# Two gate projections turned token-major, weight units placed by 64 bytes, and three steps of the attention stage reordered, in a two-layer hybrid decoder trunk

## The reference

```
y_mla   = attention of latents (softmax, causal), v 128 wide a head
y_mlstm = sigmoid(mo) * head_norm(h_ml, mlstm_norm_g)      # mo: 512 columns of z
y_ret   = silu(rg)    * head_norm(h_rt, ret_norm_g)        # rg: 512 columns of z
merged  = sum over the 3 branches b of gate[b] * (y_b @ w_br_b)
out     = merged @ w_out
```

## Time and profile before

| | us |
|---|---|
| median of 3 runs | 1314.21 |
| lowest, highest | 1313.94, 1314.42 |
| the profiled execution | 1314.52 |
| its span, first to last instruction | 1312.2 |

### The profile page before, as it was taken

One profiled execution on the slowest core, in us unless ns is written; L12 is line 12 of the kernel. 1 busy time (PEld: TensorE's weight loads), 2 busy tenths in 40 slices (PEclk: granted clock), 3 DMA queues, 4 the chain that ended last, 5 costly groups with the idle time before them and its releaser, 6 DMA issues.

```text
span 1312.2 us, 19330 instructions
## 1 busy us (share of the span) xinstructions
PE 1299.0 (99%) x8365; PEld 1178.1 (90%) x8365; DVE 889.7 (68%) x1078; ACT 637.9 (49%) x654; POOL 69.5 (5%) x59
## 2 busy tenths in 40 slices
PE   8999999999999999999999999999999999999998
PEld 8888889999999998888898888899999998988886
DVE  6666667998755676556675666779976656766555
ACT  5444446585534354444454444456754344544441
POOL 0398000000000000000000000000000000000000
PEclk9999999999999999999999999999999999999999
DMA  8755556544556555555556655556445564555562
GB/s 292 239 187 184 187 185 176 181 128 131 161 191 191 164 173 181 192 192 192 165 188 192 192 189 187 166 165 193 129 129 173 181 193 161 181 187 185 188 193 94
DMA packets 180341, 234.85 MB, mean 179 GB/s; under 512 B 7905, under 2 KB 154977, under 8 KB 180129
## 3 DMA queue, kind: packets, MB, share of 16 engines
q1 hardware_dynamic: 179872, 231.78, 55.5%
q0 software_dynamic: 240, 1.71, 0.4%
q10 hardware_dynamic: 144, 0.13, 0.1%
HBM read 232.56 MB, written 1.05 MB: 178 GB/s over the span
## 4 chain that ended last, share of the span: by engine, by line
PE 94%; DVE 3%; ACT 2%; issue 0%; DMA 0%; DVEq 0%
PE ps L1429 22%; PE ps L1418 22%; PE ps L1344 10%; PE ps L1343 10%; PE ps L1342 10%; PE ps L1417 10%; PE ps L1407 5%; PE ps L1421 1%; DVE wlo L802 1%; PE ps L1364 1%; PE ps L1376 1%; ACT whi L511 1%; PE ps L1624 1%; DVE ml_qk L974 0%; ACT rot_sw L597 0%; ACT sc L611 0%
## 5 line engine op out<-in xcount | busy, mean ns | idle before, releaser
L802 DVE TENSOR_TENSOR wlo<-raw,whi 128x2048 fp32r<-128x2048 f32 (+1 forms) x218 | 491.9, 2272 | 191.1 <-ACT whi L511 191.0
L511 ACT ACTIVATE whi<-raw 128x2048 fp32r<-128x2048 f32 (+1 forms) x218 | 413.2, 1897 | 293.8 <-DMA raw<-ffn_w_gate 113.4
L1418 PE MATMUL ps<-xpair,whi 128*128 128x512 f32 x1216 | 423.9, 395 | 0.0
L1417 PE MATMUL ps<-xpair,wlo 128*128 128x256 f32 x1064 | 299.2, 281 | 0.0
L1342 PE MATMUL ps<-xpair,whi 128*128 128x256 f32 (+1 forms) x928 | 261.5, 282 | 0.0
L1344 PE MATMUL ps<-xpair,wlo 128*128 128x256 f32 (+1 forms) x928 | 259.3, 279 | 0.0
L1343 PE MATMUL ps<-xpair,whi 128*128 128x256 f32 (+1 forms) x928 | 259.1, 279 | 0.0
L1418 PEld LDWEIGHTS ps<-xpair,whi 128*128 128x128 f32 x1216 | 221.1, 188 | 42.1
L1417 PEld LDWEIGHTS ps<-xpair,wlo 128*128 128x128 f32 x1064 | 199.6, 188 | 7.0
L1343 PEld LDWEIGHTS ps<-xpair,whi 128*128 128x128 f32 (+1 forms) x928 | 173.9, 187 | 0.5
L1342 PEld LDWEIGHTS ps<-xpair,whi 128*128 128x128 f32 (+1 forms) x928 | 173.7, 187 | 0.3
(11 more groups left out here) (234 smaller groups left out, 1572.1 us busy)
## 6 DMA issues: line engine op xcount, KB each, us to landing
raw<-w_in SPq DMA_DIRECT2D x60, 1024.0 KB, 5.2
raw<-ffn_w_down SPq DMA_DIRECT2D x44, 1024.0 KB, 4.9
raw<-ffn_w_gate SPq DMA_DIRECT2D x43, 1024.0 KB, 5.4
raw<-ffn_w_up SPq DMA_DIRECT2D x43, 1024.0 KB, 5.4
raw<-w_br SPq DMA_DIRECT2D x12, 1024.0 KB, 5.0
raw<-w_out SPq DMA_DIRECT2D x8, 1024.0 KB, 4.9
raw<-mla_w_uq SPq DMA_DIRECT2D x4, 576.0 KB, 3.9
raw<-mla_w_ukv SPq DMA_DIRECT2D x2, 1024.0 KB, 4.8
```

The lines of the kernel that those rows point to most:

```text
L511: act.activation(whi[:, n % RING, 0:size_of(n)], raw[:, n % RING, 0:size_of(n)], ACT.Copy).then_inc(w_hi, 1)
L802: dve.tensor_tensor(w_low(n), raw[:, n % RING, 0:size_of(n)], whi[:, n % RING, 0:size_of(n)].bitcast(F32), ALU.subtract).then_inc(w_lo, 1)
L1417: pe.matmul(ps[:, bank, 0:SEQ], wl[:, kk, cols], xhi[:, kk, :], start=False, stop=False)
L1418: last = pe.matmul(ps[:, bank, :], wh[:, kk, cols], xpair[:, kk, :, :], start=kk == 0, stop=kk == KC - 1)
```

## The change

1. `raw`/`wlo` and `whi` become flat rings with 64 bytes to spare, and a function gives each unit an offset of 0 or 64 bytes (`SHIFT`, 16 floats). The operands that were set 64 bytes off (`hhi` and its like, and `mhi`) lose their offsets, so that all of x's parts lie at 0 modulo 128; `raw` and `whi` begin at 64 as before. An offset of 64 bytes puts a unit at 0. It is given to the mixer's units 0, 1, 16 to 21 and 40 to 43, and to all FFN units but the first two of each layer.
2. As a shifted unit reaches 64 bytes into the next slot, some loads wait for unit n-4 instead of n-5: seven in each layer, FFN unit 5 and mixer units 17, 18, 19, 40, 42, 43.
3. mo and rg are projected token-major, each as two halves of the rows, with the sigmoid and the silu after the second half. The gate is multiplied into `hn` before the turn, and after it `gain_out` multiplies by the gain and splits, straight from PSUM.
4. In the attention stage `qn1` is copied before the rope part is swapped, and the values of token tile 1 come before those of tile 0; `pt_copy(0)` and `pt_copy(1)` go ahead of the silu; `lo(m0 + 16)` goes behind `rotate(2)`.

```diff
-LINE = 64
+LINE, ROW, SHIFT = 64, 512, 16
...
-    r_raw = region(4 * RING * UNIT)
-    raw, wlo = place("raw", [P, RING, UNIT], F32, r_raw), place("wlo", [P, RING, UNIT], F32R, r_raw)
-    whi = sb("whi", [P, RING, UNIT], F32R)
-    region(LINE)
+    r_raw = region(4 * RING * UNIT + ROW)
+    raw, wlo = (place(name, [P, RING * UNIT + SHIFT], dt, r_raw) for name, dt in (("raw", F32), ("wlo", F32R)))
+    whi = sb("whi", [P, RING * UNIT + SHIFT], F32R)
...
-    hhi = place("hhi", [P, 2 * SEQ], F32R, r_u2 + 448 + 4096)
+    hhi = place("hhi", [P, 2 * SEQ], F32R, r_u2 + 4096)
...
-    mlo = place("mlo", [P, KC, SEQ], F32R, r_y + LINE + 12288)
+    mlo = place("mlo", [P, KC, SEQ], F32R, r_y + 12288)
...
+    def shift_of(n):
+
+        k = n % U_LAYER - MIX_BASE
+        if 0 <= k < U_MIX:
+            return SHIFT if k < 2 or 16 <= k < MIX_FIXED or k >= U_MIX - MIX_OUT else 0
+        return 0 if k in (-MIX_BASE, 1 - MIX_BASE) else SHIFT
+
+    def unit(ring, n, lo=0, size=None):
+
+        at_n = n % RING * UNIT + shift_of(n) + lo
+        return ring[:, at_n:at_n + (size or size_of(n))]
+
+    def freed_by(n):
+
+        meets_next = n % RING < RING - 1 and shift_of(n) > shift_of(n - RING + 1)
+        return n - RING + 1 if meets_next else n - RING
...
-                sp.wait_ge(w_used, done_no(n - RING))
+                sp.wait_ge(w_used, done_no(freed_by(n)))
...
-                    if c == C_RV:
+                    if c in (C_RV, C_MO, C_RG):
                         load_half(l, m + i, c, i)
...
             act.wait_ge(w_used, done_no(m0 + 10))
+            copy(flat(q_nope[:, 2:4, :]), "qn1").then_inc(q_copied, 1)
             act.wait_ge(rotated, l * 6 + 1)
             swap("qr", 32).then_inc(rot_copied, 1)
-            copy(flat(q_nope[:, 2:4, :]), "qn1").then_inc(q_copied, 1)
...
+            pt_copy(0)
+            pt_copy(1)
             act.wait_ge(conv_tap, l * 32 + 32)
             act.activation(ml_qk[:, 4:8, :], ml_qk[:, 4:8, :], ACT.Silu).then_inc(qk_silu, 1)
 
-            pt_copy(0)
-            pt_copy(1)
...
             hi(m0 + 22)
-            act.wait_ge(w_used, done_no(m0 + 18))
-            copy(flat(mo[:, 0:2, :]), "mo0", func=ACT.Sigmoid).then_inc(mo_ready, 1)
-
             hi(m0 + 23)
             act.wait_ge(w_used, done_no(m0 + 19))
-            copy(flat(mo[:, 2:4, :]), "mo1", func=ACT.Sigmoid).then_inc(mo_ready, 1)
+            for t in range(TT):
+                gates(mo, t, f"mo{t}", ACT.Sigmoid).then_inc(mo_ready, 1)
...
-                last.then_inc(h_ready, 1)
-
-            def gate_out(n):
+                last.then_inc(h_normed, 1)
+                dve.wait_ge(mo_ready if n < 2 else rg_ready, l * 2 + 2)
+                dve.wait_ge(h_normed, l * 4 + (n + 1))
+                gates = (mo if n < 2 else rg)[:, 2 * (n % 2):2 * (n % 2) + 2, :, :].rearrange("p h t d -> p (h t d)")
+                dve.tensor_tensor(hn[:, n, :], hn[:, n, :], gates, ALU.mult).then_inc(h_ready, 1)
+
+            def gain_out(n):
+
                 dve.wait_ge(h_turned, l * 4 + (n + 1))
...
-            lo(m0 + 16)
 
             y_mla(0)
             scores(2)
...
             rotate(2, rq[:, 0:2, :], cos_r, sin_r)
+            lo(m0 + 16)
             lo(m0 + 17)
...
-            for t in range(TT):
+            for t in (1, 0):
                 if t == 0:
                     pe.wait_ge(rot_copied, l * 6 + 2)
                 else:
...
-            pe.wait_ge(rot_copied, l * 6 + 5)
-            project(18, "mo0")
+            pe.wait_ge(rot_copied, l * 6 + 6)
+            values_half(18, ("mo0", "mo1"), 0)
...
-            pe.wait_ge(rot_copied, l * 6 + 6)
-            project(19, "mo1")
+            values_half(19, ("mo0", "mo1"), 1)
...
-            project(20, "rg0")
+            values_half(20, ("rg0", "rg1"), 0)
             pe.wait_ge(h_scaled, l * 4 + 4)
             ret_values(1)
-            project(21, "rg1")
+            values_half(21, ("rg0", "rg1"), 1)
```

More of the change, by code:

```diff
@@ L135, in build @@
     xf = sb("xf", [P, KC, SEQ])
+    r_rows, r_y, r_b, r_qk, r_rq, r_rk = (region(n) for n in (3072, 24576, 15360, 8192, 4096, 4096))
+    r_u2, r_mv = region(22656), region(4 * TT * HEADS * (DH + 1))
     stats = sb("stats", [P, TT, 2, 6])
@@ L170, in build @@
     pt = place("pt", [P, 2, 384], F32, r_u2 + 19584)
[L171 to L176, removed]
+    row_i = place("row_i", [HEADS, SEQ], F32, r_b + 5120)
+    row_f = place("row_f", [HEADS, SEQ], F32, r_b + 6144)
+    row_t = place("row_t", [HEADS, SEQ], F32, r_rows)
+    rows_all = place("rows_all", [P, 2 * SEQ], F32, r_rows + 1024)
     row_m = rows_all[0:HEADS, :]
@@ L304, in w_low @@
     def w_low(n):
-        return wlo[:, n % RING, 0:size_of(n)]
+        return unit(wlo, n)
+    def shift_of(n):
[9 more added lines that the diff above has]
+        return n - RING + 1 if meets_next else n - RING
+    for n in range(1, N_UNITS):
+        assert n % RING == 0 or shift_of(n - 1) <= shift_of(n)
     def nth_ffn(l, w):
@@ L376, in load @@
             if n >= RING:
-                sp.wait_ge(w_used, done_no(n - RING))
-            sp.dma_start(raw[:, n % RING, 0:int(np.prod(shape))].rearrange("p (a b) -> p a b", a=shape[0]), src)\
+                sp.wait_ge(w_used, done_no(freed_by(n)))
+            sp.dma_start(unit(raw, n).rearrange("p (a b) -> p a b", a=shape[0]), src)\
               .then_inc(w_loaded[n % RING], 16)
@@ L771, in hi_half @@
         def hi_half(n, half):
-            part = slice(half * UNIT // 2, (half + 1) * UNIT // 2)
+            part = half * UNIT // 2, UNIT // 2
             act.wait_ge(w_loaded[n] if half else half_loaded[n], 16)
-            act.activation(whi[:, n, part], raw[:, n, part], ACT.Copy).then_inc(w_hi if half else half_hi, 1)
+            act.activation(unit(whi, n, *part), unit(raw, n, *part), ACT.Copy).then_inc(w_hi if half else half_hi, 1)
         act.dma_start(cst[:, 0:2 * P], a["consts"][:, 0:2 * P]).then_inc(square_loaded, 16)
@@ L1110, in head_norm @@
                                              hsd[:, n, k:k + 1], ALU.subtract, ALU.mult)
[L1111 to L1115 removed]
+                last.then_inc(h_normed, 1)
[4 more added lines that the diff above has]
+            def gain_out(n):
                 dve.wait_ge(h_turned, l * 4 + (n + 1))
[L1117 to L1119 removed]
                 for i in range(2):
[L1121 to L1126 removed]
+                    hd = 2 * (n % 2) + i
+                    src, g = ps[:, BANK[f"hT{n}"], i * SEQ:(i + 1) * SEQ], par_col(l, "ml_g" if n < 2 else "rt_g", hd)
+                    last = dve.tensor_scalar(yhi[:, 1 + n // 2, hd, :], src, g, None, ALU.mult)
+                last.then_inc(y_hi, 1)
+                dve.wait_ge(y_hi, l * 6 + (n + 3))
+                for i in range(2):
+                    hd = 2 * (n % 2) + i
+                    src, g = ps[:, BANK[f"hT{n}"], i * SEQ:(i + 1) * SEQ], par_col(l, "ml_g" if n < 2 else "rt_g", hd)
+                    last = stt(ylo[:, 1 + n // 2, hd, :], src, g, ALU.mult, yhi[:, 1 + n // 2, hd, :].bitcast(F32),
+                               ALU.subtract)
+                last.then_inc(y_lo, 1)
             def ret_probs(h):
@@ L1271, in mixer @@
                     if b == 0:
-                        gate_out(2 * h)
-                        gate_out(2 * h + 1)
+                        gain_out(2 * h)
+                        gain_out(2 * h + 1)
                     dve.wait_ge(w_used, done_no(m0 + 24 + 6 * b + 3 * h))
@@ L1311, in lo_half @@
                 dve.wait_ge(w_hi, done_no(n))
-            dve.tensor_tensor(w_low(n)[:, part], raw[:, n, part], whi[:, n, part].bitcast(F32),
+            dve.tensor_tensor(unit(wlo, n, *part), unit(raw, n, *part), unit(whi, n, *part).bitcast(F32),
                               ALU.subtract).then_inc(w_lo if half else half_lo, 1)
@@ L1346, in slot @@
         def slot(n, width):
-            return tuple(t.rearrange("p (k n) -> p k n", n=width) for t in (whi[:, n % RING, 0:size_of(n)], w_low(n)))
+            return tuple(t.rearrange("p (k n) -> p k n", n=width) for t in (unit(whi, n), w_low(n)))
         def turn_rows(stage, t):
```

56 lines of the change are left out of this document (22 added, 34 removed).

## The result

The changed kernel takes 1307.28 us (median of 4, 1307.05 to 1307.59), against 1314.32 us for the kernel before on the same chip: a ratio of 0.9944, 95% interval [0.9933, 0.9955]. The gain is 7.0 us. Forecast were 13.4 us, with a range that reached to 1309.0.

The account below looks back on a forecast made before the run. TensorE, busy 1299.0 of 1312.2 us, bounds the kernel, so time is the sum of its matmul pitches. Gains 7.9 + 1.2 + 0.6 + 1.7 + 2.0 = 13.4 us give 1301.0 us; range 1297.5 to 1309.0.

Parts of the forecast that it names:

- The case with 0.70 of the chance: Whole kernel: everything goes as forecast, 1297.5 to 1303 us; chance 0.70.
- the partial case: Whole kernel: 256-wide half costs more, half the matching gain is missing, or attention only trades waits; 1303 to 1307; chance 0.12.
- placement does nothing: Rival: pitches depend on something else, such as banks written; only attention and fewer matmuls gain, 1312.0 us; chance 0.10.
- Both at 64: Rival: 512-wide matmuls are fast only with both operands at 64, so down units lose; 1318.8 us; chance 0.08.
- Gate and up: FFN gate and up units: 1216 matched 512-wide matmuls each gain 6.5 ns, 7.9 us in all.
- The price I set at nothing: Gate/up pairs: matched 256-wide matmul taken as unchanged, bounded by 2.3 ns dearer and 4.4 ns cheaper.
- mv, rv, output: Existing token-major mixer units become matched, 1.2 us; the output product gains 0.6 us.
- mo and rg: Eight mixer units: 48 matmuls of 256 become 24 matched ones of 512, 0.21 us each, 1.7 us.
- Attention: Attention stage: reordering removes waits, 1.0 us a layer, 2.0 us in all.
- (b): Attention, mla_values(0): copies put ahead of the silu remove a wait of 0.67 us a layer.
- (c): Attention, mla_turn(2): moving a lo behind lets probs(2) end earlier, removing a 0.74 us wait a layer.
- Step (a): Attention, after unit 11's keys: removes a 0.43 us wait but delays q_rope, losing about 0.5 us a layer.

Follow-up runs that it names:

- e1: Changed kernel with the four moves of the attention stage undone; 1310.12 us, ratio 0.9965.
- e3: Changed kernel with each gate/up bank run as eight 512-wide steps, then eight 256-wide ones, instead of alternating; 1307.02 us, ratio 0.9942.
- e12: e8 with the grouping over a whole gate or up unit: sixteen 512-wide steps, then sixteen 256-wide ones; 1294.11 us, ratio 0.9839.
- e2: Changed kernel with ring slots 128 bytes further apart and the FFN's gate and up units left unmatched with x; 1301.04 us, ratio 0.9896.
- e5: Changed kernel with everything from the transposed input onward moved up by 256 bytes, weight rings unmoved; 1307.37 us, ratio 0.9947.
- e10: e6 with the high ring moved by 256 bytes in place of 128; 1307.45 us, ratio 0.9945.
- e7: Changed kernel with one move undone: the copy of qn1 again behind the copies of the rope swap; 1307.59 us, ratio 0.9948.
- e6: Changed kernel with the ring of high halves moved up by 128 bytes against the raw/low ring; 1301.68 us, ratio 0.9904.
- e8: Changed kernel, high/low halves 128 bytes apart for mixer 256-wide units, together for token-major; gate/up low half unmatched, banks grouped as e3; 1293.84 us, ratio 0.9842.
- e11: Kernel before the change, with only the high ring moved 128 bytes further from the low ring; 1303.93 us, ratio 0.9920.
- e4: e3 on the ring with slots 128 bytes further apart, gate/up high half matched with x, low half not; 1299.63 us, ratio 0.9886.

## Why the prediction was right and where it failed

*Right in sign and inside the range; 6 us off in size.* The case with 0.70 of the chance, 1297.5 to 1303, did not come. What came, 1307.28 us, is the edge of the partial case, to which I gave 0.12, and it lies in the range because the range was drawn to hold two of its parts together. The stages give 1.7 us (FFN), 1.7, 1.0 and 2.8 us where 7.9, 1.8, 1.7 and 2.0 were forecast; without the attention stage's 0.8 us too much the miss would be larger.

The rival "placement does nothing" (1312.0) is out: e1 has no move and is 4.3 us under before, of which that rival leaves room for 0.5, and x-loading 512-wide steps went from 233.4 to 228.0 ns where nothing but places changed. The Trainium skill's rule (TensorE: Matmul & The Clock Gate, Step-by-step: what each phase is for), by which the loading takes nothing from the running matmul, leaves no room for a pitch that hangs on the two operands' places, and the measured 233.4 and 228.0 ns decide against it as a guide to placement; that it is the loading which slows the stream was not shown. "Both at 64" is out too: the down steps stand at 227.0 with both operands at 0.

*Gate and up, the term that failed.* I wrote "I take 6.5 ns, as rows 3 are the thing itself". The rv unit's gain was carried to a 512-wide step that stands between two 256-wide ones. Measured, a bank of eight pairs fell from 2814 to 2798 ns, 2.0 ns a pair: 1216 x 2.0 = 2.4 us, not 7.9. e3 shows that the matched x stream does reach 227 in an unbroken run, so the place was read rightly; what failed is carrying that pitch to a 512-wide step that stands next to 256-wide ones, which does not keep it (e3, e12). In the terms of the forecast, the split of the earlier trace rows into 0.94 and 7 x 0.234 gave all the excess to the 512-wide steps' place, when a part of it belongs to their neighbours. The mean of 2.0 ns is itself made of unlike parts: against before, the four banks of an FFN step change by -13, -50, +25 and -27 ns. These sums say where it happens, not why; e2, with gate and up unmatched and the rings 128 bytes apart, has the same 2797 ns a bank as after. The cause within the alternating banks stays open.

Another 0.7 us of the 2.4 is lost elsewhere in the FFNs. The price I set at nothing, a matched 256-wide step, was in its bounds: in the pair it became cheaper, 119.6 to 116.2 ns, and in unbroken runs it is 119.8, the 0.120 of the earlier trace rows, against 117.8. The latter had no term at all: the last up unit of each of the four FFNs has 48 such steps, and it went from 5.66 to 5.74 us, 0.35 us in all. The rest is in the token-major 256-wide steps at the two ends of an FFN (0.4 us).

*mv, rv, output: hit.* 1.8 us forecast, 1.7 measured.

*mo and rg, 1.7 forecast, 1.0 measured.* Units 19 to 21 gained 0.16 to 0.20 us each, near the 0.21. Unit 18 gained nothing (+0.04), and 0.25 of the 0.33 us that are missing in each layer are there. The price after was right, the price before was not the unit's own: 5.65 us was read from unit 22, and unit 18, in both layers, is one of the few that ran at 113.3 ns a step in the kernel before, 317.74 - 312.21 = 5.53 us:

```profile
312.21 0.36 PE L1342 MATMUL ps<-xpair,whi 128*128 128x256 f32 x1
...
317.74 0.39 PE L1609 MATMUL ps<-ml_v,sc 128*128 128x129 f32 x2
```

At 5.58 us token-major there was nothing left to gain.

*Attention, 2.0 forecast, 2.8 measured.* The steps (b) and (c) are confirmed, their waits are gone. Step (a) was right in mechanism and too dear: the wait on `q_rope` came, 0.77 us long,

```profile
260.35 0.49 PE L1605 MATMUL ps<-k_nope,q_nope 128*128 128x128 f32 x2 [0.77 <-DVE q_rope L1006]
```

where "about 0.9" stood, but unit 11 grew by 0.30 us, not 0.50. Of the other 0.2 us a layer, unit 13 has 0.21: it runs at 113.3 ns a step after and ran at 117.8 before. In the first layer unit 12 lost as much, fast before and not after, with the pause before `mla_turn(1)`, 0.19 us, gone in exchange. Nothing in the change aims at this, and in e5 and e10, with the same order, it is partly unit 15 that is fast; that part of the 2.8 us is luck. And e7 shows that beside tile 1's going first the move of the copy is a gain: without it TensorE waits 0.89 us for `qn1` itself.

*Covers.* The later loads, the extra multiplication of VectorE and the later sigmoid cost nothing: no wait for any of them appears, and the busy times of the groups in the earlier trace rows answer to within 0.4 us.

## What to carry to other kernels

Read a pitch in the order in which it will stand: a step between two of another width is another operation than one in an unbroken run, and a gain seen in the one does not carry to the other. When two matmul streams of one shape differ by some per cent, compare all their addresses modulo 256, not 128 alone, and try a move of one buffer by 128 bytes before any reordering: here it was worth more than the whole change, on the kernel as it was. And where steps seem to gain by being grouped, look at the first steps of what follows; the cost may only have moved.

## What the runs showed of the hardware

- 256-column fp32r steps with x streamed and high, high and low weights loaded in turn, 64 bytes off x: 117.5 ns with the high and low half 0 or 256 bytes apart modulo 512 (after, e10), 113.5 ns at 128 (e6, e8, e11, and all slots of e2). x moved by 256 changes nothing (e5). At a distance of 0 a few whole units run at 113.3 ns all the same, three of 70 before and two of 62 after.
- 512-column steps, all matched modulo 128: 227 ns with the moving high half, the low half and the loaded operand together modulo 256 (e8: high half at 256 modulo 512, low half at 0 or 256, loaded operand at 256), 230.3 for the high half in down units when it stands 128 off (e6); the low half, not moved there, keeps 227.2 in mv, rv, mo and rg. 233 with streamed and loaded operand 64 bytes apart (before).
- 256-column steps leave 3.1 to 3.8 ns each, as a mean over an FFN step or a run, to be paid by the following 512-column steps (e3, e8, e12); in single places of e8 it is from 9 to 40 ns behind eight of them.
- What in the chip does this stays open. The runs changed places and order, and not, for instance, the writes of ScalarE, VectorE and the DMA queues into the same buffers. The padded runs e2 and e4, where slots stand 128 bytes apart modulo 512, have 512-column pitches that do not settle along a down unit (226 to 233 ns in e2), and that was not followed further.
